# Attention work ahead of the low split, inner norm roots on GpSimd, and a reordered opening, in a four-layer kernel on one core

## The reference, cut to what matters

```python
# first block, per layer: group norm of the mixer's output
yg = y.reshape(bsz, length, SSD_GROUPS, D_SSD // SSD_GROUPS)
yg = yg * lax.rsqrt(jnp.mean(yg * yg, axis=-1, keepdims=True) + RMS_EPS)
...
# second block, differential attention
s = jnp.where(key_pos[None, :] <= qpos[:, None], s, NEG)
p = jax.nn.softmax(s, axis=-1)
a = p[:, :, 0] - lam * p[:, :, 1]
return jnp.einsum("bhqk,bhkv->bhqv", a.astype(v.dtype), v)
...
o = rms_norm_2(o, subln_g) * (1.0 - lambda_init)
...
# convolution branch
h = jax.nn.silu(layer_norm(h, ln_g, ln_b))
```

## Time and profile before

| | |
|---|---|
| median of 3 runs | 1765.27 us (1764.46 to 1765.59) |
| the profiled execution | 1764.93 us, span 1762.9 us |
| TensorE (PE) busy | 1709.6 us, 97% of the span |
| vector engine (DVE) busy | 1340.2 us, 76% |
| ScalarE (ACT) busy | 921.5 us, 52% |
| GpSimd (POOL) busy | 30.8 us, 2% |
| DMA | 300.92 MB, 171 GB/s on average |
| granted TensorE clock | 0.50 from 11.74 to 15.15 us and from 35.63 to 39.05 us, else 1.00 from 4.91 to 1755.95 us |

### The profile page before, as it was taken

The page is one execution under the profiler, slowest core; times in us unless marked ns, Lnnn a source line. Parts: engine busy times, 40 slices in busy tenths (PEclk is TensorE's granted clock), DMA queues, the critical chain, the costliest instruction groups (busy, mean ns, idle before and its releaser), DMA issues.

```text
span 1762.9 us, 30277 instructions
## 1 busy us (share of the span) xinstructions
PE 1709.6 (97%) x12334; PEld 1580.0 (90%) x12342; DVE 1340.2 (76%) x2227; ACT 921.5 (52%) x1481; POOL 30.8 (2%) x51
## 2 busy tenths in 40 slices
PE   7999999999999999999999999999999999999997
PEld 6999889998999979999898998899989989989996
DVE  5867777777877867777798878866678988886666
ACT  5566555555656646555544654444344466453442
POOL 0000000000000000000000001000000000100000
PEclk9999999999999999999999999999999999999999
DMA  6544445555545445555465444555546635455552
GB/s 209 165 144 144 167 146 189 191 185 162 168 145 156 140 164 188 194 186 192 150 215 186 134 154 162 184 191 191 188 147 201 204 122 172 130 197 185 190 191 96
DMA packets 234055, 300.92 MB, mean 171 GB/s; under 512 B 6179, under 2 KB 199357, under 8 KB 233917
## 3 DMA queue, kind: packets, MB, share of 16 engines
q1 hardware_dynamic: 233609, 298.87, 52.0%
q10 hardware_dynamic: 308, 0.12, 0.0%
HBM read 293.72 MB, written 1.05 MB: 167 GB/s over the span
## 4 chain that ended last, share of the span: by engine, by line
PE 76%; DVE 17%; ACT 4%; issue 2%; DMA 0%; ACTq 0%; POOL 0%; DVEq 0%; POOLq 0%
PE bank L489 16%; PE bank L491 16%; PE bank L490 16%; DVE weights_lo L1420 7%; PE bank L567 5%; PE bank L568 5%; PE bank L569 5%; PE bank L539 2%; PE bank L540 2%; PE bank L541 2%; DVE conv_sums L1842 2%; ACT weights_hi L1017 1%; PE bank L689 1%; ACT pair L1280 1%; PE bank L594 1%
## 5 line engine op out<-in xcount | busy, mean ns | idle before, releaser
L489 PE MATMUL bank<-input_hi,weights_hi 128*128 128x256 f32 x2768 | 790.9, 286 | 12.8 <-DVE weights_lo L1420 6.5
L490 PE MATMUL bank<-input_lo,weights_hi 128*128 128x256 f32 x2768 | 783.7, 283 | 0.0
L491 PE MATMUL bank<-input_hi,weights_lo 128*128 128x256 f32 x2768 | 783.5, 283 | 0.0
L1420 DVE TENSOR_TENSOR weights_lo<-raw_weights,weights_hi 128x1024 fp32r<-128x1024 f32 (+1 forms) x554 | 649.8, 1214 | 138.3 <-ACT weights_hi L1017 136.1
L1017 ACT ACTIVATE weights_hi<-raw_weights 128x1024 fp32r<-128x1024 f32 (+1 forms) x554 | 546.3, 1036 | 331.8 <-PE bank L491 175.0
L489 PEld LDWEIGHTS bank<-input_hi,weights_hi 128*128 128x128 f32 x2768 | 531.1, 192 | 21.5 <-issue 17.7
L490 PEld LDWEIGHTS bank<-input_lo,weights_hi 128*128 128x128 f32 x2768 | 531.5, 192 | 1.8
L491 PEld LDWEIGHTS bank<-input_hi,weights_lo 128*128 128x128 f32 x2768 | 531.3, 192 | 0.0
L567 PE MATMUL bank<-weights_hi,hidden_hi 128*128 128x512 f32 x432 | 168.9, 391 | 0.2
L568 PE MATMUL bank<-weights_lo,hidden_hi 128*128 128x512 f32 x432 | 168.7, 390 | 0.0
L569 PE MATMUL bank<-weights_hi,hidden_lo 128*128 128x512 f32 x432 | 168.1, 389 | 0.0
(11 more groups left out here) (256 smaller groups left out, 1795.9 us busy)
## 6 DMA issues: line engine op xcount, KB each, us to landing
raw_weights<-in_w_in SPq DMA_DIRECT2D x105, 1024.0 KB, 5.3
raw_weights<-in_w_ff SPq DMA_DIRECT2D x64, 1024.0 KB, 5.3
raw_weights<-in_w_ffn_up SPq DMA_DIRECT2D x44, 1024.0 KB, 5.1
raw_weights<-in_w_ffn_down SPq DMA_DIRECT2D x22, 1024.0 KB, 5.0
raw_weights<-in_w_out SPq DMA_DIRECT2D x16, 1024.0 KB, 5.1
raw_weights<-in_w_o SPq DMA_DIRECT2D x8, 1024.0 KB, 5.1
pair<-pair SPq DMA_DIRECT2D x64, 64.0 KB, 2.9
raw_weights<-in_w_diff_out SPq DMA_DIRECT2D x4, 1024.0 KB, 5.1
```

What stands on the lines that cost most here:

```text
L489: mm(o, w_hi, x_hi, start=first, stop=False, skip_group_check=quiet)
L490: mm(o, w_hi, x_lo, start=False, stop=False, skip_group_check=quiet)
L491: return mm(o, w_lo, x_hi, start=False, stop=last, skip_group_check=quiet)
L1420: tt(wlo[:, t, r], raw[:, s, r], whi[:, t, r].bitcast(f32), SUB).then_inc(w_ready, 1)
```

## The change

Four edits are made together.

1. In the second block the vector engine's `extras(c)` is cut in two. `probabilities(c)` holds the mixing, the reciprocals, the masking and the copy of a head's result; from slot 15 on it runs ahead of `split_lo(c + 2)` instead of behind it. In slot 14 it stays behind.
2. `CONV_OPS` hands out the taps in other numbers: 15 to 17 get 2 instead of 3, 18 gets 4, 19 gets 8 instead of 9, 20, 22, 24 get 8 instead of 7, 23 gets 8 instead of 4, 25 gets 5 instead of 3, so that 5 are left for slot 26 instead of 11.
3. `rsqrt_diagonals` keeps its first and its last step; the root between is taken on GpSimd by one power instruction of 2 or 8 columns (`spread_roots`), with a semaphore each way. GpSimd's queue gets these 12 instructions in the order in which they come due.
4. At the opening the two parameter transposes stand behind the token transposes of layer 0, the first fillers are 20 instead of 16, the four fillers behind the parameter transposes are gone, and the fillers between the two halves of the token transposes are 10 instead of 2 in that layer.

```diff
-CONV_OPS = {4: 7, 5: 4, 6: 4, 7: 4, 8: 4, 9: 9, 10: 8, 11: 4, 12: 4, 13: 4, 14: 2, 15: 3, 16: 3, 17: 3, 18: 3, 19: 9, 20: 7,
-            21: 10, 22: 7, 23: 4, 24: 7, 25: 3}
+CONV_OPS = {4: 7, 5: 4, 6: 4, 7: 4, 8: 4, 9: 9, 10: 8, 11: 4, 12: 4, 13: 4, 14: 2, 15: 2, 16: 2, 17: 2, 18: 4, 19: 8, 20: 8,
+            21: 10, 22: 8, 23: 8, 24: 8, 25: 5}
...
-            keep_clock(16, ring[3])
+            keep_clock(20, ring[3])
             pe.wait_ge(ident_loaded, 16)
-            pe.wait_ge(rows_loaded, 16 * N_ROW_DMAS)
-            for l in range(DEPTH):
-                last = nc.tensor.transpose(ring[0][:, l * P:(l + 1) * P], prow[:, 3 * l, :], ident)
-            last.then_inc(pt_ready, 1)
-            keep_clock(4, ring[3])
...
-                turned(l * 2)
+                turned(l * 2, 10 if l == 0 else 2)
+                if l == 0:
+                    pe.wait_ge(rows_loaded, 16 * N_ROW_DMAS)
+                    for i in range(DEPTH):
+                        last = nc.tensor.transpose(ring[0][:, i * P:(i + 1) * P], prow[:, 3 * i, :], ident)
+                    last.then_inc(pt_ready, 1)
...
+            def spread_roots(k, n):
+
+                pool.wait_ge(spread_var, k + 1)
+                nc.gpsimd.tensor_tensor(small[:, 24:24 + n], small[:, 16:16 + n], minus_half[:, 0:n], ALU.pow).then_inc(spread_root, 1)
...
-            for r in range(1, 2 * DEPTH - 1):
-                roots(r)
-            pool.wait_ge(y_done, HEADS // 2 * DEPTH)
-            pool.memset(prow2[:], 0.0).then_inc(rows2_zero, 1)
+            for k in range(4 * DEPTH):
+                if k and k % 4 == 0:
+                    roots(k // 2 - 1)
+                    roots(k // 2)
+                if k == 4 * DEPTH - 1:
+                    pool.wait_ge(y_done, HEADS // 2 * DEPTH)
+                    pool.memset(prow2[:], 0.0).then_inc(rows2_zero, 1)
+                spread_roots(k, TOK)
...
             for l in range(DEPTH):
+                spread_roots(4 * DEPTH + 2 * l, 8)
+                spread_roots(4 * DEPTH + 2 * l + 1, TOK)
                 for m in range(4):
...
-            def rsqrt_diagonals(sums, n, scale, signal):
-
-                v, y, t = small[:, 16:16 + n], small[:, 24:24 + n], small[:, 32:32 + n]
-                chain(ts(v, sums, scale, EPS, MUL, ADD))
...
-                for _ in range(3):
-                    chain(tt(t, y, y, MUL))
...
+            def rsqrt_diagonals(k, sums, n, scale, signal):
+
+                y = small[:, 24:24 + n]
+                ts(small[:, 16:16 + n], sums, scale, EPS, MUL, ADD).then_inc(spread_var, 1)
+                dve.wait_ge(spread_root, k + 1)
                 for i in range(n):
                     last = ts(diag[:, i, :], ident, y[:, i:i + 1], None, MUL)
                 last.then_inc(signal, 1)
...
-                def extras(c):
+                def probabilities(c):
+
                     m, late = divmod(c - FIRST_BLOCK, 2)
                     if 0 <= c - FIRST_SCORES - 1 < 4:
                         diff_mix(c - FIRST_SCORES - 1)
...
+                    if 0 <= c - FIRST_SCORES - 3 < 4:
+                        h = c - FIRST_SCORES - 3
+                        dve.wait_ge(pv_done, l * 12 + h + 1)
+                        V.tensor_copy(ob[h // 2][:, h % 2, :], acc[3][:, 0:SEQ]).then_inc(ob_ready, 1)
+
+                def extras(c):
+                    m, late = divmod(c - FIRST_BLOCK, 2)
+                    if c == FIRST_SCORES:
+                        probabilities(c)
...
+                    if c > FIRST_SCORES:
+                        probabilities(c)
                     split_lo(c + 2, cx)
```

More of the change, by code:

```diff
@@ L235, in build @@
         small = sb("small", [P, 64])
-        minus_half = small[:, 63:64]
+        minus_half = small[:, 56:64]
+        spread_var, spread_root = ctx.enter_context(nc.semaphore("spread_var")), ctx.enter_context(nc.semaphore("spread_root"))
         one_hot = sb("one_hot", [P, 32], f32r)
@@ L594, in keep_clock, with turned @@
                     mm(b[:, :], zt[:, 0:P], zt[:, :], start=True, stop=True, skip_group_check=True)
-            def turned(r):
+            def turned(r, fillers=2):
                 def turn(t, k):
@@ L605, in turned @@
                         turn(0, k)
-                keep_clock(2, ring[3])
+                keep_clock(fillers, ring[3])
                 for b in range(4):
@@ L952, in roots @@
                     pool.wait_ge(var_ready, r * 2 + t + 1)
-                    nc.gpsimd.tensor_tensor(norm_small[:, 3, t:t + 1], norm_small[:, 2, t:t + 1], minus_half, ALU.pow).then_inc(root_ready, 1)
+                    nc.gpsimd.tensor_tensor(norm_small[:, 3, t:t + 1], norm_small[:, 2, t:t + 1], minus_half[:, 0:1], ALU.pow).then_inc(root_ready, 1)
+            def spread_roots(k, n):
+                pool.wait_ge(spread_var, k + 1)
+                nc.gpsimd.tensor_tensor(small[:, 24:24 + n], small[:, 16:16 + n], minus_half[:, 0:n], ALU.pow).then_inc(spread_root, 1)
             pool.wait_ge(half_ready, 1)
@@ L1433, in both @@
                 return x.unsqueeze(1).to_broadcast([P, 2, SEQ])
-            def rsqrt_diagonals(sums, n, scale, signal):
-                v, y, t = small[:, 16:16 + n], small[:, 24:24 + n], small[:, 32:32 + n]
-                chain(ts(v, sums, scale, EPS, MUL, ADD))
[L1439 to L1444, removed]
-                for _ in range(3):
-                    chain(tt(t, y, y, MUL))
-                    chain.sync()
-                    chain(tt(t, t, v, MUL))
-                    chain.sync()
-                    chain(stt(out=y, in0=t, scalar=1.5, in1=y, op0=ADD, op1=MUL))
-                    chain.sync()
+            def rsqrt_diagonals(k, sums, n, scale, signal):
+                y = small[:, 24:24 + n]
+                ts(small[:, 16:16 + n], sums, scale, EPS, MUL, ADD).then_inc(spread_var, 1)
+                dve.wait_ge(spread_root, k + 1)
                 for i in range(n):
@@ L1633, in group_rsqrt @@
                     dve.wait_ge(gstat, l * 4 + g + 1)
-                    rsqrt_diagonals(acc[2 + g % 2][:, 0:TOK], TOK, 1.0 / 256, gdiag)
+                    rsqrt_diagonals(l * 4 + g, acc[2 + g % 2][:, 0:TOK], TOK, 1.0 / 256, gdiag)
                 def group_scale(g):
@@ L1909, in extras @@
                         tt(hidl[:, 4 + k, :], acc[3][:, 0:SEQ], hidh[:, 4 + k, :].bitcast(f32), SUB).then_inc(moba_ready, 1)
-                    if 0 <= c - FIRST_SCORES - 3 < 4:
-                        h = c - FIRST_SCORES - 3
-                        dve.wait_ge(pv_done, l * 12 + h + 1)
-                        V.tensor_copy(ob[h // 2][:, h % 2, :], acc[3][:, 0:SEQ]).then_inc(ob_ready, 1)
                     if c == 23:
                         dve.wait_ge(ostat, l + 1)
-                        rsqrt_diagonals(acc[0][:, 0:8], 8, 1.0 / P, odiag)
+                        rsqrt_diagonals(4 * DEPTH + 2 * l, acc[0][:, 0:8], 8, 1.0 / P, odiag)
                     if c == 27:
@@ L1975, in _ @@
                 dve.wait_ge(cstat, l + 1)
-                rsqrt_diagonals(acc[2][:, 0:TOK], TOK, 1.0 / CONV_CH, cdiag)
+                rsqrt_diagonals(4 * DEPTH + 2 * l + 1, acc[2][:, 0:TOK], TOK, 1.0 / CONV_CH, cdiag)
                 gated(29)
```

## The result

The changed kernel takes 1748.78 us (median of 4 runs, 1748.60 to 1749.25) against 1765.36 us (1764.46 to 1765.59) for the kernel before, run beside it: a ratio of 0.9907, 95% interval 0.9894 to 0.9919, so 16.6 us faster. The profiled execution took 1749.25 us, 15.7 us less than the profiled execution before; its span is 1747.4 us, 15.4 less. That lies inside the predicted range of 1748.0 to 1756.4 and 3.0 us under the predicted 1751.8.

A forecast was written before the change was run, and what follows sets the result against it. In slots 15 to 18 a ring through the engines, no single engine, was taken as the bound. Terms -8.7 - 1.1 - 1.5 - 1.6 - 0.6 = -13.5 us from 1764.93, plus 0.34 for the median, gave 1751.8 us; range 1748.0 to 1756.4.

The forecast's parts named there:

- Order in the slot: Second-block attention: with mixing and masking ahead of the low split, TensorE's waits at L798 and L819 go, -8.7 us.
- the ring: Slots 15 to 18: exponentials, high split, low split, mixing and masking follow each other, 8.55 us a turn; TensorE waits.
- Taps: Convolution: six taps a layer move from slot 26 to earlier slots, removing a 0.75 us wait; -1.5 us.
- Roots, two columns: Group norms: GpSimd's power replaces 13 vector instructions, the trip is at most 1.3 us, the L705 wait goes; -1.6 us.
- Roots, eight columns: Slot 23's norm: a power of 0.55 to 1.0 us gives -1.1 us; beyond 1.6 us the wait returns.
- Opening: Kernel start: first gemm 2.1 us earlier, 1.5 us lost to a half-clock stretch; net -0.6, bounds -2.1 and +0.8 us.
- no stretch at half clock behind 15: Sign at the first gemm, expected at 15.1 us: if no such stretch follows, the forecast was too cautious at the opening.
- The clock holds: Rival, chance 0.14: no half-clock stretch at the first gemm and the one at 35.63 doesn't return; 1748.6 us.
- Slow power: Rival, chance 0.08: in slot 23 the 8-column power takes 3.0 us and TensorE waits 1.4 us; 1755.6 us.
- Split becomes the wait: Rival, chance 0.12: over-full vector engine makes gemms wait for the low split in slots 18 to 21; 1756.2 us.
- slower: Rival, chance 0.03: the split queues behind waits for TensorE's work in some 20 slots of two layers; one microsecond makes 1771.8.
- nothing in the attention: Rival, chance 0.03: something else holds TensorE's attention scores at the same moment, so the change does nothing there; 1760.5 us.

The follow-up runs named there:

- the doubled power: Changed kernel with the 8-column power computed twice on GpSimd, the first result unused: 1751.93 us, ratio 0.9928.
- the opening alone: Kernel before with only the reordered opening (transposes and fillers): 1763.72 us, ratio 0.9992.
- eight-run repeat with fillers: Changed kernel with ten more filler matmuls behind the parameter transposes, run on two chips: 1748.44 us, then 1747.30 us; eight runs together 1747.8 us.

## Why the prediction was right, and what was mis-sized

**Order in the slot.** Right in mechanism, and within the slot to the tenth. The prediction had, from the gemm's end, mask done and copy started at 4.15, split at 4.5, taps ended at 7.6; the rows show 4.16, 4.49 and 7.64. A turn fell to the slot's matmuls, 7.74 us. Undoing the order brought the waits of the earlier trace rows back and 10.6 us with them, and made alone it gave 8.9. With the new order in slots 15 to 18 alone nearly all of the gain stayed, so the ring was the cause. The term was 8.7 and measured 9.6 in gemm ends. The terms were taken from idle time, and each of these eight stalls cost 0.06 to 0.23 us beyond it, since matmuls ahead of a stall are counted as busy for longer (slot 19: 6.96 before, 6.73 after, with the same 57).

**Taps.** Right: no wait is left, -1.64 us for -1.5, and the old table costs 1.9 (1.65 by its gemm ends; the rest is within the spread of its runs).

**Roots, two columns.** The wait at L705 went, but the term was mis-sized, 1.6 for 2.44 us. 0.2 us of the difference was stall beyond idle, and 0.3 us a layer was the fourth group's stall, seen only in the weight loads. The trip itself took 0.97 us (189.09 to 190.06), which was the price read off the opening for one column: the power took 0.70 instead of 0.55, the hand-overs 0.11 instead of 0.27. The opening's other power says the same: its row has 0.67 us of idle, 0.12 beyond the power, where the prediction took the 0.82.

**Roots, eight columns.** The size of the instruction was wrong: 1.65 us instead of 0.55 to 1.0, near the middle of the bounds from 0.55 to 3.0. The addition of eight columns (0.20 us) says nothing about a power, whose cost grows with the columns. The prediction said that beyond 1.6 us the wait would come back. It didn't: the first step came at 4.13 instead of 4.2 (1010.36 - 1006.23), the hand-overs took 0.12 us instead of 0.27, and the next instruction stood 1.57 us behind the start of the diagonals, not 1.66. The edge lies at about 1.65 + 0.1 us, and the doubled power, which is beyond it, costs nearly its whole length, 3.1 us for two times 1.61. So the term held, 1.22 for 1.1, by about a tenth of a microsecond. The Trainium skill's 2.6 cycles an element, from "GPSIMD Engine Reference", 3.1, is for additions; here a further column of a power cost 0.15 to 0.16 us, and the measurement decides. The trade itself was good: one power for 13 small vector instructions, 1.93 us against 2.46 at eight columns.

**Opening.** The net came out as forecast, -0.53 for -0.6, but this is in part luck, and two smaller misses offset each other. The gemm started at 15.33, 1.9 us earlier for the forecast 2.1, after 2.54 us of idling (2.7 forecast). The prediction had the first fillers end at 7.84 and so the token transposes begin there; they began at 8.50, while in this profile full clock is first recorded at 6.46 us, against 4.91 in the one before. The half-clock stretch fell on the gemm and took 1.4 us, 1.5 forecast. Whether it falls there changes from execution to execution: it does in five of the eight profiles with the new opening and no further fillers, among them one of the two of the changed kernel itself. The expected stretch was thus no safe term, and the sign "no stretch at half clock behind 15" came up in three profiles. Over the eight the first gemm ends at 22.20 us on average (21.71 to 22.80, and the changed kernel's first profile is the 22.80), over the four with the old opening at 23.36 (22.88 to 24.24): -1.2 us, about what the opening alone gave. The mean, not one profile, was the number to forecast. The bound of +0.8 counted seven more fillers at half clock; the edit adds eight (30 against 22), which makes it +1.0.

The sum's 0.34 us for the median over the profiled execution had the wrong sign: after, the median lies 0.47 us below the profiled execution. The other executions have no profile, so that the clock did this is likely but not shown.

**The rivals.** *The clock holds* gave the nearest number, 1748.6, but its account fell. It counted 1.7 us for the stretch at 35.63 not coming back. It also counted 1.5 us for a first gemm at full clock, which holds in three of the eight profiles and not in the changed kernel's first. The stretch at 35.63 is absent in that one, and nothing was gained by that: the gemm end of chunk 3 is 2.0 us earlier and that of chunk 5 only 0.54, because the wait for the low split grew from 0.47 to 1.73 us. There the chain that makes the low split sets the pace, not TensorE, as the constant 31.5 us to the end of chunk 5 shows. *Slow power* fell on the size, 1.65 us for 3.0, while its mechanism is what the doubled power shows. *Split becomes the wait* and *slower* fell on TensorE's waits, where none for the split stands in the attention, and *nothing in the attention* on the order alone, which gave 8.9 us.

**The 3.0 us between 1751.8 and 1748.8** are: 1.9 in the gemm ends (stalls beyond idle, and the hidden one), 0.3 behind the last of them and around the span, and 0.8 in how the medians lie to the profiled executions.

What stays open: why the eight-run repeat with fillers splits into runs near 1747.3 to 1747.8 and near 1749.0. The clock could do it, but only two of the runs have a profile. Open, too, is what pauses the vector engine at the mask in the kernels with the new roots and the old order.

## What to carry to other kernels

When a ring through three engines bounds a slot, put the ring's steps ahead of throughput work whose deadline is later, and check each slot's sum of the moved engine, not its average. Price a stall by the difference of ends, and look at the weight loads too: idle in the matmul view was a lower bound here (12.9 us of idle, 14.9 us in the gemm ends). A stretch at half clock was only worth removing where TensorE set the pace; look at the next wait behind it before counting it. And where such a stretch moves from one execution to the next, take several profiles before giving it a term of the sum.

## What the runs showed of the hardware

- A power on GpSimd over 128 partitions took 0.55 us for one column, 0.70 for two and 1.65 for eight, while an addition of eight took 0.20.
- The hand-overs from the vector engine to GpSimd and back cost 0.12 us beyond the power of eight columns and 0.11 beyond that of two, less than the 0.27 read off the opening at one.
- The same program had half-clock stretches at 16.71 us in one execution and at 34.38 and 1293.90 us in another. The first made the gemm under it 1.36 us longer (7.47 against 6.11). The second cost nothing. The third made the opening of the last layer 0.7 us longer (49.46 against 48.72 us over the same seven chunks).
- With 2.54 us of idling ahead of the first gemm, a half-clock stretch fell on it in five of eight profiles; with 0.39 us, in none of two.
- A stall cost 0.06 to 0.23 us more than TensorE's idle time at it, and one of 0.31 to 0.32 us left only 0.04 us of idle in the matmul view, with 0.46 at the weight load.
